# Strassen's form for the gate, up and down products of a feed-forward block, with the activation kept in DRAM between two stages

## What is computed

```
def swiglu(h, w_gate, w_up, w_down):
    return (jax.nn.silu(h @ w_gate) * (h @ w_up)) @ w_down
...
    x = x + rms_norm(mix, norm_mix_post[l])
    f = swiglu(rms_norm(x, norm_ffn_pre[l]), w_gate[l], w_up[l], w_down[l])
    x = x + rms_norm(f, norm_ffn_post[l])
```

## Time and profile before

| | |
|---|---|
| median of 3 runs | 2086.68 us (2086.66 to 2087.96) |
| span of the profiled execution | 2084.9 us |
| TensorE busy | 2050.2 us |
| VectorE, ScalarE, GpSimd busy | 936.7, 554.3, 191.4 us |
| mean granted TensorE clock | 0.996 |
| moved by DMA | 176.66 MB |

### The profile page before, as it was taken

How to read it: one execution, slowest core, us unless ns; L and a number is a source line. 1 busy time by engine, 2 the same in 40 slices (tenths; PEclk the granted TensorE clock), 3 DMA queues, 4 the chain that set the end, 5 groups by cost and what they waited for, 6 DMA issues and landing times.

```text
span 2084.9 us, 25821 instructions
## 1 busy us (share of the span) xinstructions
PE 2050.2 (98%) x10384; PEld 1703.7 (82%) x10384; DVE 936.7 (45%) x1313; ACT 554.3 (27%) x1079; POOL 191.4 (9%) x187
## 2 busy tenths in 40 slices
PE   8999999999999999999999999999999999999996
PEld 6888888878888888888888888888888888888885
DVE  6554444464553334433344334653344433444246
ACT  6444444543342011211112111321111211112112
POOL 2222222210001000000000000330000000000004
PEclk9999999999999999999999999999999999999998
DMA  6111110356677101111111111741111110111122
GB/s 223 41 45 46 40 40 30 127 182 210 209 234 249 51 31 60 60 40 46 34 60 60 40 43 57 279 145 40 33 48 60 60 40 29 52 60 60 40 81 101
DMA packets 114578, 176.66 MB, mean 85 GB/s; under 512 B 4592, under 2 KB 82416, under 8 KB 114544
## 3 DMA queue, kind: packets, MB, share of 16 engines
q1 hardware_dynamic: 114544, 176.19, 25.0%
HBM read 134.23 MB, written 41.94 MB: 84 GB/s over the span
## 4 chain that ended last, share of the span: by engine, by line
PE 94%; DVE 3%; DMA 2%; ACT 1%; SPq 0%; issue 0%; POOL 0%; DVEq 0%; ACTq 0%
PE ZB L971 11%; PE ZB L973 11%; PE ZB L972 11%; PE ZA L971 11%; PE ZA L972 11%; PE ZA L973 11%; PE S L971 4%; PE S L973 4%; PE S L972 4%; PE T L973 4%; PE T L971 4%; PE T L972 4%; DVE acc L927 1%; PE S L1090 1%; PE S L1060 1%; PE T L981 1%
## 5 line engine op out<-in xcount | busy, mean ns | idle before, releaser
L971 PE MATMUL ZA<-h2T_hi,gu_hi 128*128 128x512 f32 x704 | 273.9, 389 | 0.9 <-DMA h2T_lo<-h_d 0.9
L971 PE MATMUL ZB<-h2T_hi,gu_hi 128*128 128x512 f32 x704 | 273.9, 389 | 0.0
L972 PE MATMUL ZA<-h2T_lo,gu_hi 128*128 128x512 f32 x704 | 273.9, 389 | 0.0
L973 PE MATMUL ZB<-h2T_hi,gu_lo 128*128 128x512 f32 x704 | 273.9, 389 | 0.0
L972 PE MATMUL ZB<-h2T_lo,gu_hi 128*128 128x512 f32 x704 | 273.9, 389 | 0.0
L973 PE MATMUL ZA<-h2T_hi,gu_lo 128*128 128x512 f32 x704 | 273.9, 389 | 0.0
L677 ACT ACTIVATE th<-ZA 128x512 f32<-128x512 f32 x44 | 26.3, 598 | 706.5 <-PE ZA L973 706.5
L909 DVE SCALAR_TENSOR_TENSOR sil<-th,ZA 128x512 f32<-128x512 f32 x44 | 30.2, 687 | 319.3 <-ACT th L677 319.3
L971 PEld LDWEIGHTS ZA<-h2T_hi,gu_hi 128*128 128x128 f32 x704 | 132.1, 188 | 28.6 <-issue 1.1
L909 DVE SCALAR_TENSOR_TENSOR sil<-th,ZB 128x512 f32<-128x512 f32 x44 | 30.3, 688 | 278.3 <-ACT th L677 278.3
L973 PEld LDWEIGHTS ZB<-h2T_hi,gu_lo 128*128 128x128 f32 x704 | 132.1, 188 | 27.5
(11 more groups left out here) (161 smaller groups left out, 3714.7 us busy)
## 6 DMA issues: line engine op xcount, KB each, us to landing
raw_a<-w_gate SPq DMA_DIRECT2D x22, 1024.0 KB, 5.5
raw_b<-w_up SPq DMA_DIRECT2D x22, 1024.0 KB, 7.8
raw_a<-w_down SPq DMA_DIRECT2D x22, 1024.0 KB, 4.9
h_d<-h2s SPq DMA_DIRECT2D x30, 512.0 KB, 5.1
xt<-x SPq DMA_DIRECT2D x16, 512.0 KB, 3.4
mix_d<-mix SPq DMA_DIRECT2D x16, 512.0 KB, 2.6
mixin<-mix_d SPq DMA_DIRECT2D x16, 512.0 KB, 6.2
xres<-x SPq DMA_DIRECT2D x16, 512.0 KB, 6.2
```

The source lines that it names most:

```text
L971: e.matmul(out_ap, lhi, rhi, start=start, stop=False)
L972: e.matmul(out_ap, lhi, rlo, start=False, stop=False)
L973: return e.matmul(out_ap, llo, rhi, start=False, stop=stop)
```

## The change

Each of the three large products is cut into 2 x 2 blocks and computed by Strassen's form in Winograd's variant: seven block products of sums and differences of the blocks, in place of eight.

*Gate and up.* The token block of 1024 is cut into tiles of even and odd number, the 1024 input columns into two halves. For a pair of token tiles the four quarters and four sums of them lie in `quarters` (copies on ScalarE, pair_sums on VectorE), and seven S parts, unsplit, are stored by h2_store in one transfer for two tiles, in runs of 512 bytes. They are loaded per block of 1024 tokens (load_s) and split when they are in SBUF. w_gate and w_up are laid out on the host as w_gu by groups and quarters; load_t fetches the four quarters of one half (gate is u = 0, up is u = 1), GpSimd makes the four T sums (t_sums), ScalarE and VectorE split all seven. A half is seven products of 12 matmuls, into four PSUM banks of its own; products 5 to 7 are added in PSUM to products 1, 2 and 4, and so they wait until ScalarE has copied product 1 and 2 out (copies, p1 and p5) and VectorE has added up u2 and u3 (chain). The four result blocks are v22 (GpSimd, corner), bank 0, v12 and v21 (VectorE). silu and gated make the activation's four blocks, group_end the four sums, and act_store writes seven 512-column parts to act_d in DRAM (1.84 MB, runs of 512 bytes).

*Down.* A stage of its own behind all 22 groups: seven products (i) over 8 tile pairs (m), 56 steps of 33 matmuls, alternating between T0 and T1. For each step load_sb fetches 704 KB of act_d, ScalarE and VectorE split it (sb_hi, sb_lo), and VectorE's drain adds the result into y, which now holds the 16 tiles in SBUF. The weight side of each product (tb) is 2.9 MB, and for i = 1 to 4 sums are made in place (tb_sums with tb_sub, of the same size). drain of step 0 and every load_sb from step 2 on wait until the last act_store has landed. Tiles of odd number are complete after the fifth product (i = 4), those of even number in the seventh, and they are normalized and stored during products i = 5 and 6.

Beside this the kernel's arrays in SBUF start at a lower address, and a scratch area for DMAs is set to 1024 bytes. The mixing half's products are as before.

```diff
+A11, A12, A22, L1, L2, L3, L4 = range(7)
+B12, B22, B11, B21, R3, R1, R2, R4 = range(8)
+UP_PRODUCTS = [(A11, B11), (L1, R1), (L2, R2), (L3, R3), (A12, B21), (L4, B22), (A22, R4)]
+DOWN_PRODUCTS = [A11, L2, L3, A22, L1, L4, A12]
...
-            def group(n, b):
-                for q in range(4):
-                    h, f = q // 2, q % 2
-                    if h == 0:
-                        e.wait_ge(gate_split, 2 * n + f + 1)
-                        e.wait_ge(up_split, 2 * n + f + 1)
-                    if not (isinstance(n, int) and n == 0 and h == 0):
-                        e.wait_ge(gu_drained[f], 2 * n + h)
-                    e.wait_ge(h2T_in[h], 32 * (b + 1))
-                    for a in range(2):
-                        for c in range(KD):
-                            ins = three(GU[f][:, a, :], gu_hi[f][:, a, c, :], gu_lo[f][:, a, c, :],
-                                        h2T_hi[h][:, c, :], h2T_lo[h][:, c, :], c == 0, c == KD - 1)
-                    ins.then_inc(gu_full[f], 1)
...
+            def up_half(n, g, u, first, begin):
+                for i, (s, t) in enumerate(UP_PRODUCTS):
+                    if i == 0 and not begin:
+                        e.wait_ge((sil_done, act_done)[u], 4 * g)
+                    if i < 3:
+                        e.wait_ge(t_split, 3 * n + i + 1)
+                    if first and u == 0:
+                        e.wait_ge(s_split, 7 * (0 if begin else 1) + i + 1)
+                    if begin and i == 0 and u:
+                        e.wait_ge(y_done, TILES)
+                    if begin and i == 2:
+                        if u:
+                            e.wait_ge(quarter_done, 2 * TILES)
+                        else:
+                            e.wait_ge(y_done, TILES - 1)
+                    if i in (4, 5):
+                        e.wait_ge(pcopy_done, 2 * n + i - 3)
+                    if i == 6:
+                        e.wait_ge(u3_done, n + 1)
+                    bank = GU[u][i if i < 4 else (0, 1, 3)[i - 4]]
+                    for k in range(HK):
+                        w = slice(k * P, (k + 1) * P)
+                        hi, lo = t_hi[u][:, t - 1, w], t_lo[u][:, t, w]
+                        e.matmul(bank, hi, s_hi[i][:, k, :], start=i < 4 and k == 0, stop=False, skip_group_check=True)
+                        e.matmul(bank, hi, s_lo[i][:, k, :], start=False, stop=False, skip_group_check=True)
+                        ins = e.matmul(bank, lo, s_hi[i][:, k, :], start=False, stop=k == HK - 1, skip_group_check=True)
+                    ins.then_inc(prod_done, 1)
...
+            def down(it, par, first):
+                e.wait_ge(sb_split, it + 1)
+                if not first:
+                    e.wait_ge(y_added, it - 1)
+                for k in range(NG):
+                    ins = three(DN[par], sb_hi[par][:, k, :], sb_lo[par][:, k, :], tb_hi_of[:, k, :],
+                                tb_lo_of[:, k, :], k == 0, k == NG - 1)
+                ins.then_inc(dn_done, 1)
...
+            def h2_store(j):
+                e.wait_ge(sums_done, 4 * j + 4)
+                e.dma_start(h2_d[j // BP, :, :, :, (j % BP) * P:(j % BP + 1) * P].rearrange("p s k n -> p (s k) n"),
+                            quarters[:, 1:8, :].rearrange("p s (k n) -> p (s k) n", n=P)).then_inc(h2_out, 16)
...
+            def load_t(n):
+                if n >= 2:
+                    e.wait_ge(prod_done, 7 * n - 8)
+                e.dma_start(t_raw[n % 2][:, 0:4, :], w_gu[n // 2 % NG, n % 2, :, :, :]).then_inc(t_in[n % 2], 16)
+            def act_store(g):
+                e.wait_ge(act_sums, 4 * g + 4)
+                e.dma_start(act_d[g // NG, :, :, :, g % NG, :].rearrange("p s t n -> p (s t) n"),
+                            ac[:, 1:8, :].rearrange("p s (t n) -> p (s t) n", n=P)).then_inc(act_out, 16)
...
+            for g in range(GROUPS):
+                if g:
+                    load_t(2 * g + 1)
+                    if g == NG:
+                        e.wait_ge(prod_done, 14 * g)
+                        load_s(1, 6)
+                    act_store(g - 1)
+                if g + 1 < GROUPS:
+                    load_t(2 * g + 2)
+                if g == NG - 1:
+                    e.wait_ge(h2_out, 8 * TILES)
+                    for i in range(6):
+                        e.wait_ge(prod_done, 7 * (2 * g + 1) + i + 1)
+                        load_s(1, i)
...
+            def load_sb(it):
+                i, m = it // (TILES // 2), it % (TILES // 2)
+                if it >= 2:
+                    e.wait_ge(sb_split, it - 1)
+                e.dma_start(sb_raw[it % 2][:, :, :], act_d[m // BP, :, DOWN_PRODUCTS[i], m % BP, :, :])\
+                    .then_inc(sb_in[it % 2], 16)
...
+            for it in range(7 * TILES // 2):
+                i, m = it // (TILES // 2), it % (TILES // 2)
+                if it + 2 < 7 * TILES // 2:
+                    load_sb(it + 2)
+                if m == 0 and 0 < i < 6:
+                    e.wait_ge(dn_done, TILES // 2 * i)
+                if m == 0 and i == 0:
+                    load_tb(1, 1, 1)
+                    load_sub(1, 0, 1)
+                if m == 3 and i == 0:
+                    e.wait_ge(tb_sum, 2)
+                    load_sub(1, 0, 0)
+                if m == 0 and i == 1:
...
+            def t_sums(n, u):
+                t = t_raw[u]
+                e.wait_ge(t_in[u], 8 * (n - u) + 16)
+                e.tensor_tensor(t[:, R3, :], t[:, B22, :], t[:, B12, :], ALU.subtract).then_inc(tsum_done, 1)
+                e.tensor_tensor(t[:, R1, :], t[:, B12, :], t[:, B11, :], ALU.subtract).then_inc(tsum_done, 1)
+                e.wait_ge(tsum_done, 4 * n + 2)
+                e.tensor_tensor(t[:, R2, :], t[:, B22, :], t[:, R1, :], ALU.subtract).then_inc(tsum_done, 1)
+                if not isinstance(n, int) or n >= 2:
+                    e.wait_ge(prod_done, 7 * n - 7)
+                e.wait_ge(tsum_done, 4 * n + 3)
+                e.tensor_tensor(t[:, R4, :], t[:, B21, :], t[:, R2, :], ALU.subtract).then_inc(tsum_done, 1)
+            def corner(n, g, u):
+                e.wait_ge(pcopy_done, 2 * n + 2)
+                e.wait_ge(u3_done, n + 1)
+                if u:
+                    e.wait_ge(sil_done, 4 * g + 1)
+                elif not isinstance(g, int) or g:
+                    e.wait_ge(act_done, 4 * g - 3)
+                e.tensor_tensor(v22[:, :], u3[:, :], p5[:, :], ALU.add).then_inc(v22_done, 1)
...
+            def t_hi_parts(n, u):
+                e.wait_ge(t_in[u], 8 * (n - u) + 16)
+                if not isinstance(n, int) or n >= 2:
+                    e.wait_ge(prod_done, 7 * n - 8)
+                e.activation(t_hi[u][:, 0:3, :], t_raw[u][:, 1:4, :], ACT.Copy).then_inc(t_hi_done, 1)
+                e.wait_ge(tsum_done, 4 * n + 2)
+                e.activation(t_hi[u][:, 3:5, :], t_raw[u][:, 4:6, :], ACT.Copy).then_inc(t_hi_done, 1)
+                e.wait_ge(tsum_done, 4 * n + 4)
+                e.activation(t_hi[u][:, 5:7, :], t_raw[u][:, 6:8, :], ACT.Copy).then_inc(t_hi_done, 1)
             tile2(0, 0, 0, 0, True)
...
+            def copies(n, u):
+                e.wait_ge(prod_done, 7 * n + 1)
                 if not isinstance(n, int) or n:
-                    e.wait_ge(dn_full[3], 4 * n)
-                e.wait_ge(down_in, 16 * n + 16)
-                e.activation(flat(wd_hi[:, :, :]), raw_a[:, :], ACT.Copy).then_inc(wd_hi_done, 1)
-            def group(n, more=True):
-                unit(n, 0)
...
+            def pair_sums(j):
+                e.wait_ge(quarter_done, 4 * j + 4)
+                q = quarters
+                if not isinstance(j, int) or j:
+                    e.wait_ge(h2_out, 16 * j)
+                e.tensor_tensor(q[:, 4, :], q[:, 0, :], q[:, 3, :], ALU.add).then_inc(sums_done, 1)
+                e.tensor_tensor(q[:, 6, :], q[:, 1, :], q[:, 0, :], ALU.subtract).then_inc(sums_done, 1)
+                e.wait_ge(sums_done, 4 * j + 1)
+                e.tensor_tensor(q[:, 5, :], q[:, 4, :], q[:, 1, :], ALU.subtract).then_inc(sums_done, 1)
+                e.wait_ge(sums_done, 4 * j + 3)
+                e.tensor_tensor(q[:, 7, :], q[:, 2, :], q[:, 5, :], ALU.subtract).then_inc(sums_done, 1)
...
+            def chain(n, u, parts):
+                e.wait_ge(prod_done, 7 * n + 3)
+                e.wait_ge(pcopy_done, 2 * n + 1)
+                e.tensor_tensor(u2[:, :], GU[u][2], p1[:, :], ALU.add).then_inc(u2_done, 1)
+                for b, i in parts:
+                    s_lo_part(b, i)
+                e.wait_ge(prod_done, 7 * n + 4)
+                e.wait_ge(u2_done, n + 1)
+                if not isinstance(n, int) or n:
+                    e.wait_ge(v22_done, n)
+                e.tensor_tensor(u3[:, :], GU[u][3], u2[:, :], ALU.add).then_inc(u3_done, 1)
+            def upper(n, u):
+                e.wait_ge(prod_done, 7 * n + 6)
```

(110 more changed lines are left out.)

650 lines of the change are left out of this document (348 added, 302 removed).

## The result

The changed kernel takes **1945.22 us** (median; 1945.08 to 1948.16) against 2086.67 for the kernel before: a ratio of 0.9325, 95% interval 0.9312 to 0.9338. The forecast was 1940, with a range of 1905 to 1978. The profiled execution has a span of 1946.4 us, so the change took 138.5 us off the span; the forecast's sum was 146.5. This execution is the slowest of the four, and the spans of the other three are 1943.3 to 1943.4: differences of whole spans against 1946.4 come out up to 3 us too large.

What follows compares the result with a forecast made beforehand. The prediction took TensorE's matmul stream to bound the kernel. It summed 2084.9 - 179.5 - 19 + 2 + 14 + 6 + 23 + 3 + 4 = 1938 us of span, with 1.8 for the median 1940 us, range 1905 to 1978.

Steps and rivals of the forecast that it cites:

- The rival of hidden turnovers: Transfers are not served in order or land sooner; 10 us or less left of the 52 extra: 1889 to 1905; chance 0.13.
- 792 matmuls less: Feed-forward part: 5544 matmuls instead of 6336 at an unchanged pitch of 226.7 ns, -179.5 us.
- mixing: Mixing stage: weight and S loads ahead of xres make it some 6 us late, +2 us (0 to 6).
- entry: Start of the feed-forward part: late S loads and splits, then p1 behind the last h2_store, +14 us (4 to 25).
- change of block: Change of token block: seven fresh S parts to split on VectorE delay a half, +6 us (1 to 12).
- up to down: Turn to the down stage: act_done wait, then load_sb(2) and load_sb(3) late in the queue, +23 us (8 to 30).
- steady down: Down products of 7.48 us each; later bursts of tb and sub and the sixth product cost +3 us (0 to 12).
- clock and short hitches in the feed-forward part: Forecast as clock: TensorE restarts at the 1.2 GHz level after two long gaps, +4 us (0 to 8).
- end: After the last matmul: a tail of 8.7 us instead of 27.8, -19 us.
- my walk through it: Steady up group, step by step: the next weights are the tightest chain, slack 5.7 us, 0 extra in 38.08 us.
- bound by its feeders: Up stage: weights, GpSimd sums and splits need 2 to 4 us more than 38.1 a group: 1984 to 2028; chance 0.13.
- the slower one: Up stage: the weight chain exceeds its time by 6.7 us a group, eating the 147 us won; chance 0.04.

Runs made afterwards that it cites:

- run 3: Kernel after, with 18 unread matmuls issued into TensorE's idle stretch before the first down product and 30 before the fourth: 1946.58 us, ratio 0.9327.
- run 4: Kernel after, with s_lo(0,1) made after tile2(14) and the first tile's t_lo in VectorE's order instead of before them: 1944.87 us, ratio 0.9318.
- runs 1: Kernel after, with load_sb(3) issued right after load_sb(2), ahead of the two loads of down weights: 1943.9 us, ratio 0.9311.
- the last: Kernel after with edits of run 2 and run 4, load_sb(2), load_sb(3) and first down product earlier, load_sub(1) behind load_sb(4), second weight block's sums later: 1932.33 us.
- run 2: Kernel after, with the last h2 store issued as two transfers and VectorE's first silu waiting only for the first: 1940.2 us, ratio 0.9295.

## Why the prediction was right, and what in it was not

The mechanism and the places were right; 1945 for 1940 is also luck, since errors of both signs met. The rival of hidden turnovers fell: TensorE waited 32.1 us in the three places behind the start of the up stage. (Its own range had a slip: 10 us or less of the 52 give 1888 to 1898, not up to 1905.) Measured from the traces, the span splits at the first matmul of the up stage (628.46 before, 634.15 after) and the last one of the down stage (2066.64 and 1937.52):

| term | forecast | measured |
|---|---|---|
| 792 matmuls less | -179.5 | -179.6, and 2.0 more that the old stream lost by itself |
| mixing | +2 | +5.7 |
| entry | +14 | +11.0 |
| change of block | +6 | +6.8 |
| up to down | +23 | +14.4 |
| steady down | +3 | 0 |
| clock and short hitches in the feed-forward part | +4 | +14.6 |
| end | -19 | -9.4 |
| sum | -146.5 | -138.5 |

The 14.6 is what remains of 1303.6 us from 634.15 to the end of the down stage after 5544 x 0.2267 = 1256.8 and 32.2 of waits. All of this is for the profiled execution; the median one is 3 us shorter, and no trace shows where.

**The stream.** The pitch held in both new stages. The group took 38.08 us, with a load of weights landed in 4.8 us, and my walk through it was close: sums 27.1 for 28, VectorE there at 30.9 for 30.6, first t_lo 32.6 for 32.4. The totals were too low: by the stretch from 690 to 1060 VectorE is busy for 26.7 us a group and GpSimd for 17.3, for 22 and 13.5, since their steps lengthen each other. The experiments show how near the feeders were: 32.7 us a group by themselves, and over the edge with four more adds of GpSimd. The rival "bound by its feeders" and the slower one were mechanisms that exist, further off than the chances feared by some 5 us a group. The slower one even named its chain, weights behind the act store. What I had wrong was the price at which slack is used up: I counted the adds one by one, while they also delay the act store, and through it the weights. The Trainium skill, SBUF — State Buffer, section SBUF: two separate sides, has the blocking itself: of a VectorE instruction with two SBUF inputs and a GpSimd one that reads SBUF, the one that starts first holds the ports for its whole length and the other waits. The rows agree: the four adds beside VectorE's t_lo and gated steps took 8.02 us, 2.0 each for 1.3, and VectorE's sums beside the next ones 1.7 for 0.69.

**The end: the step that failed.** "Today the last matmul starts at 2056.88" is false. That row was the last of the stretch that I had asked for, not of the engine. In the trace of the kernel before TensorE goes on to

```profile
2066.64 0.39 PE L973 MATMUL S<-wd_hi,act_lo 128*128 128x512 f32 x1
```

and the earlier trace rows already said so: 75 matmuls and 17.0 us busy after 2050 end at 2067, not at 2057. The old tail was 18.3 us, the new one is 8.9 (8.7 forecast), so the term is -9.4, half of -19.

**The clock: a mis-sized term.** I allowed two restarts in the feed-forward part, and four happened there (the fifth is part of the mixing's 5.7), at 2.4 to 3.0 us each and 10.6 together; the other 4.0 remain for the first matmul after each wait and for smaller hitches. That is 14.6 for 4.

**The turn: too dear.** The start at E + 5.4 (forecast 6) and the place behind the weights were right; the third product waited 1.3 for 3.5, the fourth 7.7 for 10.8, the second load_sub cost nothing for 3. The 1.3 is no faster load: the third product started 24.7 us after the last up matmul, for 24.6 forecast. It was only wanted later, since the half clock had stretched the first product by 2.5 us; run 3, with the first product at full clock, has a wait of 3.85 there. So part of what this term saved stands under the clock. The fourth product did start earlier than forecast, 40 us after E for 43. I had moved the bytes at the 355 GB/s of the earlier trace rows; here the same queue made 413, which would account for most of it, in this row of the kernel after:

```profile
1516.00:1536.00 20.00, 13.89 (x60) 10.82 (x59) 2.23 (x2) 1.58 (x2) 0.00 (x0) 0.94 1.00 413
```

**Entry and mixing.** The p1 wait came at 8.4 as worked out, while s_lo and t_lo cost 2.6 for 5.6. The mixing's loss came mainly not from a late xres, for which VectorE waited 1.08 us, but from VectorE's order: s_lo(0,0) and (0,1), put before tile 14, took 6.65 us there and held up mixT_lo of tile 15.

```profile
611.67 6.65 DVE L1018 TENSOR_TENSOR s_lo<-s_raw,s_hi 128x2048 fp32r<-128x2048 f32 x2
```

I had priced these splits by their duration and never asked what is queued behind them; run 4, which moved one of them, shows that this was the cause: the wait of 4.3 us became 1.1, and no half clock followed.

## What to carry to other kernels

Before the first and last rows of a stretch are used as an engine's first and last work, check them against a count: busy time and instructions in a stretch that reaches to the end. Give every idle stretch of TensorE of some 4 us its restart as well, and when a wait is removed at a crossing of stages, follow the in-order queues, of the DMA and of the splitting engine, to the next thing that they make late: four of the edits here (runs 1, 3, 4 and the last) gave back a third or more of their gain at another product. Slack is used up at once by every delay that meets in it: here the adds themselves and the late load that they caused. And compare medians or stages, not the span of one execution with that of another: here one of four lay 3 us above the rest.

## What the runs showed of the hardware

- In the kernel after, waits of 0.3 to 1.95 us left the clock of TensorE at 2.4 GHz, and those of 4.1 us and more brought 11 to 14 matmuls at a longer pitch, mostly 0.43 us. In between the runs differ: behind 2.4 us (680.93 of run 2) there were 7 at 0.43, behind 2.2 us (1516.40 of the same run) none. Matmuls that nobody reads, issued into the gap, prevented it.
- A GpSimd add of 512 columns lasted 1.3 us alone and up to 2.0 beside VectorE's two-input steps, and these lasted 1.7 for 0.69. GpSimd's corner sum, mostly beside a split, took 2.59 us on the average of 44.
- SyncE's queue moved 413 GB/s over 20 us of weight and act loads, more than the 355 of the fullest stretch before.
